# A fused model step on one core: the last weight tile and the first product of a stage by halves of the rows, at four changes of stage

## The reference

```python
for layer in range(2):
    mix = mixer(rms_norm(h, norm_pre))            # recurrence, then attention
    h = h + rms_norm(mix, norm_post)
    ff = relu(rms_norm(h, mlp_norm_pre) @ w_up) ** 2 @ w_down
    h = h + rms_norm(ff, mlp_norm_post)
    if layer == 0:
        k, v = split(rms_norm(h, kv_norm) @ w_kv)
h = second_block(h)                               # opens with rmsnorm(h, norm_mix) @ w_in
```

## Time and profile before

| what | us |
|---|---|
| median of three runs | 2617.7 (2615.97 to 2617.8) |
| profiled execution, its own time | 2614.55 |
| its span in the profile | 2612.7 |
| PE busy | 2532.8 |
| DVE busy | 1474.9 |
| ACT busy | 1160.1 |
| POOL busy | 155.1 |

### The profile page before, as it was taken

One profiled execution on the slowest core, in us unless ns is written; L12 is line 12 of the kernel. 1 busy time (PEld: TensorE's weight loads), 2 busy tenths in 40 slices (PEclk: granted clock), 3 DMA queues, 4 the chain that ended last, 5 costly groups with the idle time before them and its releaser, 6 DMA issues.

```text
span 2612.7 us, 31879 instructions
## 1 busy us (share of the span) xinstructions
PE 2532.8 (97%) x12440; PEld 2063.3 (79%) x12440; DVE 1474.9 (56%) x2377; ACT 1160.1 (44%) x2087; POOL 155.1 (6%) x149
## 2 busy tenths in 40 slices
PE   7999999999999999999989999999999999999998
PEld 5888778888776678888867888888877787788886
DVE  5555464334566655344368888886666566543343
ACT  4254443223356645233247666665455444442232
POOL 1110010000010000000010010000000010000000
PEclk9999999999999999999999999999999999999999
DMA  4212124435232222322323212222312243233222
GB/s 133 73 57 65 57 75 125 117 107 127 81 104 72 77 68 89 105 97 89 99 63 105 64 58 65 73 71 84 92 58 62 70 142 99 73 105 97 97 97 73
DMA packets 196790, 226.24 MB, mean 87 GB/s; under 512 B 7393, under 2 KB 132609, under 8 KB 196385
## 3 DMA queue, kind: packets, MB, share of 16 engines
q1 hardware_dynamic: 196640, 224.21, 28.2%
HBM read 214.22 MB, written 9.44 MB: 86 GB/s over the span
## 4 chain that ended last, share of the span: by engine, by line
PE 81%; DVE 11%; ACT 5%; issue 2%; DMA 0%; POOL 0%; DVEq 0%; SPq 0%; ACTq 0%; POOLq 0%
PE bank L1886 22%; PE bank L1887 22%; PE bank L1888 22%; DVE CV L2597 2%; PE bank L1892 2%; DVE wlo L2371 2%; PE bank L1893 2%; PE bank L1894 2%; PE bank L1928 1%; ACT whi L2153 1%; PE bank L1905 1%; PE bank L2085 1%; PE bank L2093 1%; PE bank L2061 1%; PE bank L1992 1%
## 5 line engine op out<-in xcount | busy, mean ns | idle before, releaser
L2371 DVE TENSOR_TENSOR wlo<-raw,whi 128x1024 fp32r<-128x1024 f32 x389 | 484.1, 1250 | 664.8 <-ACT whi L2153 662.2
L2153 ACT ACTIVATE whi<-raw 128x1024 fp32r<-128x1024 f32 x389 | 409.1, 1058 | 592.7 <-PE bank L1888 576.7
L1886 PE MATMUL bank<-XAh,whi 128*128 128x512 f32 x1536 | 614.9, 400 | 16.7 <-DVE XAl L2379 4.8
L1888 PE MATMUL bank<-XAh,wlo 128*128 128x512 f32 x1536 | 601.6, 392 | 0.0
L1887 PE MATMUL bank<-XAl,whi 128*128 128x512 f32 x1536 | 601.4, 392 | 0.0
L1886 PEld LDWEIGHTS bank<-XAh,whi 128*128 128x128 f32 x1536 | 290.2, 189 | 94.7 <-issue 28.6
L1888 PEld LDWEIGHTS bank<-XAh,wlo 128*128 128x128 f32 x1536 | 290.1, 189 | 62.3
L1887 PEld LDWEIGHTS bank<-XAl,whi 128*128 128x128 f32 x1536 | 290.6, 189 | 58.7 <-issue 0.7
L1886 PE MATMUL bank<-XBh,whi 128*128 128x512 f32 x824 | 327.8, 398 | 2.9 <-DVE XBl L2377 1.7
L1887 PE MATMUL bank<-XBl,whi 128*128 128x512 f32 x824 | 321.7, 390 | 0.0
L1888 PE MATMUL bank<-XBh,wlo 128*128 128x512 f32 x824 | 321.6, 390 | 0.0
(11 more groups left out here) (338 smaller groups left out, 3374.2 us busy)
## 6 DMA issues: line engine op xcount, KB each, us to landing
raw<-in_w_in SPq DMA_DIRECT2D x77, 512.0 KB, 3.8
raw<-in_up SPq DMA_DIRECT2D x64, 512.0 KB, 3.5
raw<-in_down SPq DMA_DIRECT2D x64, 512.0 KB, 3.6
raw<-in_a_w_in SPq DMA_DIRECT2D x32, 512.0 KB, 3.9
raw<-in_w_up SPq DMA_DIRECT2D x32, 512.0 KB, 3.7
raw<-in_w_down SPq DMA_DIRECT2D x32, 512.0 KB, 3.7
raw<-in_w_kv SPq DMA_DIRECT2D x16, 512.0 KB, 3.5
raw<-in_w_ssd_branch SPq DMA_DIRECT2D x16, 512.0 KB, 3.3
```

The source lines that it names most:

```text
L1886: pe.matmul(out, wh[:, w, c], xh[:, x, 0:s.ntok], start=st, stop=False)
L1888: m = pe.matmul(out, wl[:, w, c], xh[:, x, 0:s.ntok], start=False, stop=en)
L2153: act.activation(s.hi, s.raw, ACT.Copy).then_inc(s.whi[0], 1)
L2371: dve.tensor_tensor(s.lo, s.raw, s.hi.bitcast(F32), ALU.subtract).then_inc(s.wlo[0], 1)
```

## The change

Tile 7 is made in two halves of 256 rows (24 matmuls of 256 columns each), the second one in two pieces, with the sum for the first half between them. The factor, the first two tiles of `h` and their splits are then made half by half, and so is the first unit of the next product: for fm as two sets of 24 matmuls of 256 columns into banks that four matmuls on zeros open first, for tm as two sets of 12 matmuls of 512 columns. The `warm` matmuls at the four changes are gone. Weight splits stand later by one unit around the halved unit. The fourth change's sum of squares goes from POOL to DVE. At the start only 61 KB of the constants are loaded ahead of the first weights, tiles of `x` and weights alternate, `setup` comes later, and four matmuls on a tile of ones run while the loads do. The recurrence's first scaled tiles are issued one ahead of their splits. `wi_exp` is cut in two steps, the maximum and the exponentials, one piece apart. In the key product one piece goes ahead of `rcol`.

```diff
+            if halves and kk == 0:
+                fm = jobs[0][0] == "fm"
+                if fm:
+
+                    z = add("zeros", zero=X.lo[:, nk - 1, :], x_free=X.after, banks=taken, filled=sig("zeros.filled"), opened=sig("zeros"))
+                    X.after = X.after + [z.opened]
+                    yield
+                for x in range(2):
+                    done = [sig("unit")] if x else []
+                    add("unit", n=first, parts=parts, per=per, at=0, nk=n, kk=0, total=nk, ntok=256, c0=256 * x, outs=outs if fm else outs[2 * x:2 * x + 2], done=done,
+                        xh=X.hi, xl=X.lo, x0=x0, x_ready=list(X.ready), ends=False, begins=not fm, opened=fm, late=True)
+                    if x:
+                        p.unit_done += done * len(parts)
+                    yield
+                continue
...
+        def ones_half(bank, x):
+            add("ones", q=st["sum"], sq=st["added"], bank=bank, c0=x * 256, n=256, first=True, final=False, ones=sig("ones"))
+            t = add("ones", q=st["q"], sq=st["half"], bank=bank, c0=x * 256, n=256, first=False, final=True, ones=sig("ones")).ones
+            if x:
+                st["sum"].free(t)
+                st["q"].free(t)
+            return t
...
-        def close():
-            b = [ring_a.take(), ring_a.take()]
-            r, rt = rms_close(b, ones(b), D)
-            parts = [(HALVES[0], rt[0]), (HALVES[1], rt[1])]
-            for k in range(9):
+        def close(X, name, k0, nxt, opened, ring=ring_all, mx_free=(), plus=False):
+
+            g, fm = opened
+            bs, rb = [ring.take() for _ in range(2)], [ring.take() for _ in range(2)]
...
+            d = [sig("unit"), sig("unit")]
+            product(0, 0, 8, d[0:1])
+            mix(0, d[0])
+            tile.half(0, mx[:, 7, HALVES[0]], mt[7])
+            product(1, 0, 4, [])
+            factor(0, tile.ones_half(rb[0], 0))
+            product(1, 4, 4, d[1:2])
+            p.unit_done.append(d[1])
+            X.after = d[1:2]
+            mix(1, d[1])
+            if fm:
+                assert next(g) != WAIT
+            res = first_tiles(0)
+            tile.half(1, mx[:, 7, HALVES[1]], mt[7])
+            m = tile.ones_half(rb[1], 1)
+            for k in range(2):
+                nxt.half(k, 0, res[k])
+            factor(1, m)
+            assert next(g) != WAIT
+            for k, v in enumerate(first_tiles(1)):
+                ht[k] = v
+                nxt.half(k, 1, v)
+            assert next(g) != WAIT
+            for k in range(2, 9):
...
-                    yield k - 1
+                    v = scale(k, ALL, rt[1])
+                if k > 2:
+                    nxt(k - 1)
...
-            r.free(sc_[-1])
+                    ht[k] = residual(k, ALL, v)
+                if k in (5, 8):
+                    assert next(g) != WAIT
...
+        def half(k, x, ready):
+
+            if k == 0 and x == 0:
+                X.open()
+            c = HALVES[x]
+            X.ready[k] = sig("xlo")
+            add("xsplit", hi=X.hi[:, k, c], lo=X.lo[:, k, c], src=h[:, k, c], src_ready=ready, src2=NONE, scale=col(gain[g] + k), x_free=X.after, xhi=sig("xhi"), xlo=X.ready[k])
+            if x and early:
+                tile(hsrc(k), ht[k])
+        nxt.half = half
...
-    def tiles_and_units(tiles, nxt, g):
-
-        b = ring_all.take()
-        for k in tiles:
-            if k == 0:
-                b.free(add("warm", bank=b, n=WARM, warm=sig("warm")).warm)
-            nxt(k)
-            if k == 1:
-                assert next(g) != WAIT
-        for _ in range(2):
-            assert next(g) != WAIT
...
+    K.gain_in, K.cst_in = sig("gain_in", 16), sig("cst_in", 32)
+    load_gain, load_cst = Step(kind="load_gain", land=K.gain_in), Step(kind="load_cst", land=K.cst_in)
+    load_x = [Step(kind="load_x", k=k, land=ht[k]) for k in range(8)]
+    b, t = ring_all.take(), tmps.take()
+    s = add("first_warm", bank=b, t=t, n=4, filled=sig("filled"), warm=sig("first.warm"))
...
-            split(XB, k, hsrc(k), ht[k], scale=col(gain["a_norm_pre"] + k), src2=K.cst_in)
+            if k == 5:
+                s = add("setup", lam=sig("lam"), lb=sig("lb"), eps=sig("eps"), lam1=sig("lam1"), lam2=sig("lam2"), lb1=sig("lb1"), lb2=sig("lb2"))
+                K.lam, K.lb, K.eps = s.lam, s.lb, s.eps
+            split(XB, k, hsrc(k), ht[k], scale=col(gain["a_norm_pre"] + k), src2=K.gain_in)
...
+            rows = norm_tiles(XA, hsrc, ht, gain["a_norm_pre"], (r, rt), room=3)
+            next(g0)
+            yield
+            done = 0
+            for got in rows:
+                yield got
+                if got != WAIT:
+                    done += 1
+                    if done == 2:
+                        next(g0)
...
         f = rms_close(b, ones(b), D)
+        assert next(gk) != WAIT
         b = ring_all.take()
...
-    nxt, squares, ones = into(XB, "norm_mix_2", early=True)
+    nxt, squares, ones = into(XB, "norm_mix_2", by="sq_add_v", early=True)
...
+            f, normed = [], []
+            for x in range(4):
+                if x < 2:
+                    f.append(dict(s=ss[x], c=stw[:, 2 * hp + x, :], hd=2 * hp + x, slope=slopes[x], biased=s2.biased[x], top=sig("wi.top"), exp=sig("wi.exp")))
+                    add("wi_top", **f[x])
+                if 0 < x < 3:
+                    add("wi_exp", **f[x - 1])
+                if x > 1:
+                    normed.append(add("wi_norm", s=ss[x - 2], c=stw[:, 2 * hp + x - 2, :], exp=f[x - 2]["exp"], normed=sig("wi.norm")).normed)
...
+    order = [load_gain, p.order[0]] + loads[0] + load_x[0:2] + loads[1] + load_x[2:4] + loads[2] + load_x[4:6] + [load_cst] + load_x[6:8] + [splits[0]] + loads[NRAW]
...
+            while placed < min(s.n - bool(s.get("late")) + (NW if s.n > 1 else 2), len(splits)):
...
+        elif k == "zeros":
+            on.wait_ge(*s.filled)
+            for b in s.banks:
+                on.room(b)
+                m = pe.matmul(b.t[:, :], s.zero[:, 0:P], s.zero, start=True, stop=False)
+            m.then_inc(s.opened[0], 1)
...
+            dve.tensor_scalar(s.zero, cst[:, 0:512], 0.0, None, ALU.mult).then_inc(s.filled[0], 1)
```

More of the change, by code:

```diff
@@ L536, in evac, with product, mix, factor @@
             yield
[L538 to L542 removed]
+        def close(X, name, k0, nxt, opened, ring=ring_all, mx_free=(), plus=False):
+            g, fm = opened
+            bs, rb = [ring.take() for _ in range(2)], [ring.take() for _ in range(2)]
+            u, n = (name, k0, 8, ((7 * P, P),)), len(p.units)
+            part = tile_of(whi, n % NW, u), tile_of(wlo, n % NW, u)
+            p.units.append(u)
+            r = rrs.take()
+            rt = [None, None]
+            def product(x, at, nk, done):
+                p.pieces += 1
+                add("unit", n=n, parts=[part], per=8, at=at, nk=nk, kk=at, total=8, ntok=256, c0=256 * x, outs=[Step(job=("fm", 0), i=0, bank=bs[x], at=0)], done=done,
+                    xh=X.hi, xl=X.lo, x0=0, x_ready=list(X.ready), ends=bool(done), begins=at == 0)
+            def mix(x, m):
+                e = add("mix", mx=mx[:, 7, HALVES[x]], bank=bs[x], cols=HALVES[x], unit=m, mx_free=list(mx_free), plus=plus, mix=sig("mix"))
+                bs[x].free(e.mix)
+                mt[7] = e.mix
+            def factor(x, m):
+                rt[x] = add("rfin", bank=rb[x], ones=m, r=r, c0=x * 256, n=256, dim=D, rfin=sig("rfin")).rfin
+                rb[x].free(rt[x])
+            def scale(k, c, f):
+                return add("res_scale", mx=mx[:, k, c], mix=mt[k], gain=col(gain_of + k), r=r.t[:, c], rfin=f, scaled=sig("res.scaled")).scaled
+            def residual(k, c, v):
+                return add("residual", mx=mx[:, k, c], h=h[:, k, c], scaled=v, h_ready=ht[k], res=sig("res")).res
+            def first_tiles(x):
+                return [residual(k, HALVES[x], scale(k, HALVES[x], rt[x])) for k in range(2)]
+            d = [sig("unit"), sig("unit")]
[22 more added lines that the diff above has]
+            for k in range(2, 9):
```

137 lines of the change are left out of this document (57 added, 80 removed).

## The result

The changed kernel takes 2588.99 us (median of four runs, 2586.79 to 2590.75), the kernel before 2617.75 beside it (2615.97 to 2619.4). The ratio is 0.989, with a 95% interval of 0.9873 to 0.9907: 28.8 us less where 22.7 were forecast. The profiled execution of the changed kernel took 2590.75 (span 2589.0), that of before 2614.55 (2612.7): 23.8 us less.

The account below looks back on a forecast made before the run. PE, busy 97%, was taken to bound the kernel, with DVE's chain of tiles at changes of stage. Terms 1.0 + 2.5 + 1.0 + 3.8 + 9.6 + 4.8 = 22.7 us took 2617.7 to 2595.0, range 2586 to 2606.

Parts of the forecast that it names:

- What bounds it, and the halves at the first three changes: Changes of stage: PE's gap, then DVE's chain of tiles, bound them; 1.0, 2.5 and 1.0 us less.
- the quantity that was stepped: First three changes: end of unit 4 after tile 7's start, from stepping DVE's instructions: 34.4 from 35.43, second 34.05 from 35.70.
- Fourth change: Halves, sums of squares on DVE and less half clock together save 3.8 us, bounds 1.5 and 4.5.
- The sums' term: Fourth change: residuals lose POOL's 1.10 slowdown four times, DVE's added sums cost 3.0; 1.4 us gained.
- The third term: Fourth change: PE's half clock behind the fourth unit's start costs 1.46 us; half of it counted as gain.
- Start: Kernel start: earlier loads, filler matmuls on ones and reordered scaled tiles save 9.6 us, bounds 5 and 11.
- the third, what issuing a scaled tile ahead of the split saves: Start: scaled tiles every 1.3 us instead of 2.12 shorten PE's wait of 2.58; 2.0 us gained.
- The four copies of `Vg`: Start: the chain of scaled tiles begins behind these copies, so its reordering was put at 2.0 us.
- Attention: Windowed attention: `whi` ahead of the second head's exponentials removes 4.8 of PE's 5.3 us waits, bounds 2 and 5.3.
- the slower rival: Windowed attention: PE waits for later exponentials in all eight head pairs, 28 us lost, time 2627.8; chance 0.02.
- more than that: Whole kernel: terms near their upper bounds, 27.4 us gained, time 2590.3; chance 0.13.
- the rival (fewer warm matmuls, more half-clock stretches): Changes of stage: without `warm` matmuls, five more half-clock stretches take 7 us, time 2602.0; chance 0.08.

Follow-up runs that it names:

- the kernel with both moves: Changed kernel with residuals ahead of the previous tile's split and the two weight splits set apart, behind tiles 4 and 6: 2584.76 us.

## Why the prediction was right

- **What bounds it, and the halves at the first three changes:** right in size (0.92, 2.56, 0.94 for 1.0, 2.5, 1.0) and, at all three, in the quantity that was stepped: the four units end at 34.61, 34.20 and 34.61 after the start of tile 7, before at 35.53, 35.70 and 35.55 (34.4, 34.05 and 34.4 forecast, from 35.43 and 35.70). What was left out is the clock. At the second and third change before, the half-clock stretch fills PE's time so that it has no pause from the first unit to the fourth. One piece of the stepping at the first change was off: with 0.85 gained in the gap and 0.5 to 1 lost in the chain, tile 7's low part would come about when it did before, and it comes 1.1 later; by the rows the gain is that the fourth unit's weights are split ahead of it. At the second, 2.5 was made of 1.65 for the halves and 0.85 for the piece ahead of rcol; measured in the stretch they are 1.06 to 1.43 and 1.13 to 1.50, the lower value beside the kernel before and the upper beside the changed one. That this sum comes out so close is luck, for one part was taken too large and the other too small.
- **Fourth change:** 4.39 for 3.8. The start of the fourth unit is right (3.12 for 3.05), but its two terms were mis-sized, and the errors offset each other. Stepping gave the halves 1.65 and the sums 1.4. Alone they bring the fourth unit forward by 1.10 and 2.31, and as a second edit by 0.81 and 2.02. The sums' term missed two things that the rows show: before, the weight split that ran beside POOL took 1.58 us instead of 1.23, and one of the adds on DVE falls into a time (0.65) in which DVE had waited anyway. The third term, half of 1.46 for the half clock behind, was 1.27. It is also why the whole stretch does not add up from the runs (3.94 for the sums alone, 2.40 for the halves alone, 4.39 together): with either edit alone it is gone.
- **Start:** 11.67 for 9.6, above the upper bound of 11. The first product (8.80 for 8.3) and the ones (25.25 for 24.65) were right to 0.6, and the first product moves by that much from trace to trace. That the first 14 matmuls ran at half speed was read from their step of 0.42; the clock printed for them in the earlier trace rows is 1.00, and the profile has no record of it before 19.0 us. The step that failed is the third, what issuing a scaled tile ahead of the split saves: 2.0 forecast, 4.64 in the traces, 4.91 when undone alone. It priced PE's wait of 2.58 alone, and put at nothing the other two, 1.37 and 1.14, and the half-clock stretch behind them. The four copies of `Vg`, which were to hold the chain up, leave PE a wait of 0.74 (at 47.70).
- **Attention:** the three waits are gone, 5.3 by the view of waits, where 4.8 was taken. No other wait took their place, and the slower rival has nothing for it. In the table only 4.01 shows, as the first wait's place lies in the stretch that the clock made longer.
- **The range:** its lower end was to be 2590.3 less 3, which is 2587.3 and not 2586; the median of 2588.99 lies above both. It lies below the 2590.3 of "more than that" too, by what the clock gave.
- **The clock:** the rival (fewer warm matmuls, more half-clock stretches) did not come. The page that spoke for it, the Trainium skill's "TensorE: Matmul & The Clock Gate" (🔬 Part 1: The HAM clock gate), is borne out by the filler at the start, where it is worth 2.2 us, and not by the warm matmuls, whose return changed nothing. What the rival did not see is that the halved first unit shortens PE's pause, and with that the half-clock stretches at the first three changes are gone. The opposite of the rival came, in part: the median fell 5 us more than the pair of profiles. Windows from dt to the first transposes, of the changed kernel and of the one with the residual first:

```profile
1341.23:1884.44 543.21, 528.07 (x2888) 456.50 (x2889) 428.95 (x645) 331.03 (x706) 46.91 (x24) 0.98 0.25 74
```

```profile
1337.64:1876.41 538.77, 520.69 (x2889) 449.84 (x2890) 428.39 (x644) 331.02 (x706) 46.91 (x24) 0.99 0.25 75
```

The same instructions take 538.8 to 543.3 us, and the time goes, by and large, with how long the clock was at half (1.2 GHz) in them: 23.9 us in the first of these traces (five stretches of 3.4 and one of 6.8) and in the repeat of the changed kernel, 20.5 without halves (541.05), 17.1 in the kernel with both moves (541.77), 10.2 with the warm matmuls back (538.95) and 6.8 in the second window. Over whole runs the clock goes with the time too: before at a mean of 0.990 took 2620.0 to 2621.6, at 0.993 2612.8 to 2615.7; the changed kernel at 0.993 2590.5 to 2591.6, at 0.996 2586.6 to 2586.8. The profiled execution of before (0.992, 2614.55) was among its shorter ones, that of the changed kernel (0.993) among its longer ones. At an equal 0.993 the two differ by 21 to 25 us, as the sum said; the medians differ by 28.8 because before mostly ran at 0.991 and the changed kernel at 0.993 to 0.996. The comparison at an equal mean is rough, for a mean does not say where the half-clock stretches lie, and those at the first three changes cost almost nothing. Part of the difference in the mean is the start (2.2 us lost at half clock there, gone for good) and those stretches. How many lie in the long stretch differs between traces of the same instructions, and no run here puts a cause to that.

## What to carry to other kernels

When a chain on another engine bounds a stage, find out what stands in the chain ahead of the one result that is waited for: by the rows, a weight split that moved from behind it to ahead of it is what made the first change shorter, and reordering two instructions per tile (the residual ahead of the split of the tile before) gave 3.9 us in four places for nothing. List every wait and every half-clock stretch that an edit can remove, not only the longest wait; the third part of the start was forecast 2.6 us too small for want of that. Edits that remove the same loss must be priced together, as at the fourth change, where with either one alone the half-clock stretch was gone. Where only a few us are at stake, compare the starts of the same matmuls in two traces: at the changes of stage they agree to 0.1 or 0.2 us, while the whole time moves by 5 us with the clock. Take a repeat first, since other stretches, the start among them, move by 0.3 to 4 us.

## What the runs showed of the hardware that was not expected

- Four traces of identical work differ by 4.5 us in one stretch (538.76 to 543.25), with 6.8 to 23.9 us of it at a granted clock of 0.50, in a part where PE is 97% busy (528.07 of 543.21).
- At the first three changes of stage the clock fell to half in eight of nine places where PE had stood 2.41 to 4.23 us ahead of a product, in two of the three kernels with the `warm` matmuls in front, and in none of 33 where it stood at most 1.05 us.
- What filler matmuls at the start give depends on the pause that follows: with pauses of up to 1.92 us behind them the first product went at 0.23 us a matmul in all eleven traces, and with 4.64 us its first ten matmuls took 0.43 each, at a granted clock of 0.50. The way to the ones took 16.45 and, in the repeat, 17.31 us; its steps are 0.23 as well, and the difference is waits, for the product had started earlier (8.27) than its data came.
- A pair of warm matmuls ahead of a product moved none of the first three stretches by more than 0.02 us.
